# A two-layer streaming encoder on one core: the FFN's up product turned round, and GpSimd's preparation of the state-space matrices reordered

## The reference

```
for l in range(2):
    x = LN(alpha * x + 0.5 * swiglu(x, ffn1_w_up[l], ffn1_w_down[l]))
    x = LN(alpha * x + mixer(x, ...))            # state-space branch + sparse attention
    x = LN(alpha * x + 0.5 * swiglu(x, ffn2_w_up[l], ffn2_w_down[l]))

def swiglu(x, w_up, w_down):                     # w_up 1024 x 5632, w_down 2816 x 1024
    gate, up = split(x @ w_up, 2)
    return (silu(gate) * up) @ w_down

# state-space branch, per layer, 2048 complex states:
lam = min(lam_re, -1e-4) + i * lam_im ;  dt = exp(log_dt)
a_bar = exp(lam * dt) ;  b_bar = (a_bar - 1) / lam * b ;  c = c_re + i * c_im
states = scan(a_bar, b_bar @ u) ;  y = Re(c @ states) + d * u
```

## Time and profile before

| | |
|---|---|
| median of 3 runs | 1118.56 us (1118.28 to 1119.14) |
| profiled execution, from its first to its last instruction (span) | 1117.5 us |
| what the median has beside that span | 1.1 us |
| busy: TensorE, VectorE, ScalarE, GpSimd | 1105.8, 752.0, 561.1, 391.1 us |
| granted TensorE clock, mean | 0.999 |

### The profile page before, as it was taken

How to read it: one execution, slowest core, us unless ns; L and a number is a source line. 1 busy time by engine, 2 the same in 40 slices (tenths; PEclk the granted TensorE clock), 3 DMA queues, 4 the chain that set the end, 5 groups by cost and what they waited for, 6 DMA issues and landing times.

```text
span 1117.5 us, 17726 instructions
## 1 busy us (share of the span) xinstructions
PE 1105.8 (99%) x5979; PEld 917.9 (82%) x5979; DVE 752.0 (67%) x1073; ACT 561.1 (50%) x805; POOL 391.1 (35%) x560
## 2 busy tenths in 40 slices
PE   9999999999999999999999999999999999999997
PEld 7788888997788888888888888889877888888886
DVE  6657755789977865675575555467898787565544
ACT  6545433674873554543344544336748645453540
POOL 4889975107700188998500000011275000000001
PEclk9999999999999999999999999999999999999999
DMA  9776753644565577565367575536535666657541
GB/s 287 242 228 208 247 176 113 211 136 137 157 223 192 166 224 242 184 221 187 112 201 227 159 245 192 192 91 226 164 112 160 209 199 210 211 172 241 189 150 38
DMA packets 158655, 208.95 MB, mean 187 GB/s; under 512 B 12760, under 2 KB 107128, under 8 KB 158592
## 3 DMA queue, kind: packets, MB, share of 16 engines
q1 hardware_dynamic: 155232, 202.29, 56.7%
q10 hardware_dynamic: 2592, 3.67, 1.2%
q0 software_dynamic: 768, 2.17, 0.6%
HBM read 207.02 MB, written 1.06 MB: 186 GB/s over the span
## 4 chain that ended last, share of the span: by engine, by line
PE 82%; DVE 8%; ACT 3%; issue 3%; DMA 2%; SPq 1%; POOLq 0%; POOL 0%; DVEq 0%; ACTq 0%
PE ps L744 25%; PE ps L746 25%; PE ps L745 25%; DVE wlo L1246 4%; PE ps L768 2%; DMA raw<-in_ffn_w_up 1%; DVE score L1441 1%; ACT whi L430 1%; DMA raw<-in_w_in 1%; PE ps L758 1%; PE ps L986 1%; DVE gates L1413 1%; PE ps L1123 1%; PE ps L1125 1%; PE ps L1126 1%
## 5 line engine op out<-in xcount | busy, mean ns | idle before, releaser
L1246 DVE TENSOR_TENSOR wlo<-raw,whi 128x1024 fp32r<-128x1024 f32 (+1 forms) x371 | 475.7, 1298 | 188.4 <-ACT whi L430 174.2
L430 ACT CAST whi<-raw 128x1024 fp32r<-128x1024 f32 (+1 forms) x371 | 384.7, 1044 | 287.1 <-PE ps L746 225.2
L744 PE MATMUL ps<-whi,xh 128*128 128x512 f32 x976 | 384.4, 394 | 0.2 <-DVE wlo L1246 0.2
L746 PE MATMUL ps<-whi,xl 128*128 128x512 f32 x976 | 377.8, 387 | 0.0
L745 PE MATMUL ps<-wlo,xh 128*128 128x512 f32 x976 | 377.4, 387 | 0.0
L744 PEld LDWEIGHTS ps<-whi,xh 128*128 128x128 f32 x976 | 183.3, 188 | 39.0 <-issue 3.4
L746 PEld LDWEIGHTS ps<-whi,xl 128*128 128x128 f32 x976 | 183.2, 188 | 37.8
L745 PEld LDWEIGHTS ps<-wlo,xh 128*128 128x128 f32 x976 | 183.5, 188 | 34.9
L1671 POOL TENSOR_TENSOR rstd<-var_eps,cst 128x1 f32<-128x1 f32 x12 | 18.2, 1518 | 529.8 <-DVE var_eps L1295 520.7
L744 PE MATMUL ps<-whi,hh 128*128 128x512 f32 (+1 forms) x355 | 139.5, 393 | 0.0
L746 PE MATMUL ps<-whi,hl 128*128 128x512 f32 (+1 forms) x355 | 137.7, 388 | 0.0
(11 more groups left out here) (195 smaller groups left out, 1209.3 us busy)
## 6 DMA issues: line engine op xcount, KB each, us to landing
raw<-in_ffn_w_up SPq DMA_DIRECT2D x351, 256.0 KB, 4.0
raw<-in_ffn_w_down SPq DMA_DIRECT2D x176, 256.0 KB, 3.1
raw<-in_w_in SPq DMA_DIRECT2D x128, 256.0 KB, 3.4
raw<-in_w_branch SPq DMA_DIRECT2D x32, 256.0 KB, 3.3
raw<-in_w_out SPq DMA_DIRECT2D x32, 256.0 KB, 3.8
bias_g<-bias_rows ACTq DMA_DIRECT2D x16, 192.0 KB, 3.7
raw<-in_w_in SPq DMA_DIRECT2D x16, 148.0 KB, 2.3
affine<-in_ln_g SPq DMA_DIRECT2D x4, 512.0 KB, 5.6
```

Source lines behind the costliest of these rows:

```text
L430: nc.scalar.copy(whi[:, s % RING, 0:w], raw[:, s % RAW, 0:w]).then_inc(S["hi_done"], 1)
L744: nc.tensor.matmul(o, ah, bh, start=start, stop=False)
L746: return nc.tensor.matmul(o, al, bh, start=False, stop=stop)
L1246: nc.vector.tensor_tensor(wlo[:, s % RING, 0:w], raw[:, s % RAW, 0:w], f32(whi[:, s % RING, 0:w]), ALU.subtract).then_inc(S["split_done"], 1)
```

## The change

Three things are changed together.

1. From the third chunk on the up product has the weights as the stationary factor (`feature_chunk`). `xh` and `xl` lie next to each other as `x_hl`. A block of 128 columns of `whi` is multiplied with `xh` and `xl` at once (512 columns, the two products in the two halves of a PSUM bank), and the same block of `wlo` with `xh` alone (256 columns). The result has features in partitions, so that the transposes of h fall away in nine of eleven chunks. The two halves of a bank are added: ScalarE copies one half out (two copies), VectorE adds the other (two additions), then silu, product, high part and rest as before, on 512 elements at once. A chunk's result needs four banks, and TensorE begins chunk c when the rest of h of chunk c-2 is written (`h_split`).
2. In `prepare`, `gather_bias` stands behind the angles, b and c are loaded earlier, two quarters of b and all four of c are computed before the table, and the last two quarters of b after it. `b_bar` has two buffers. Twelve small products of the table are dropped in each layer (the squares are no longer scaled by one). VectorE's `clamp` stands at the head of the FFN, and its change of sign of c (`negate_c`) behind the third chunk instead of in the down product.
3. In the opening, the transposes of h of chunks 0 and 1 move into the third chunk, behind its first and third tile (`TURN_H`). Of the first FFN's chunk 0, both silus and both products stand ahead of the next four weight splits.

```
-                for c in range(2, PEEL):
-                    up_chunk(0, f, s0 + 4 * c, c, c % 2)
-                    h_transpose(f, c - 1, (c - 1) % 2, False)
+                for c in range(OLD_C, PEEL):
+                    feature_chunk(0, f, s0 + 4 * c, c, c % 2, c == OLD_C)
...
+            def feature_chunk(i, f, s, c, b, first=False):          # TensorE
+                if first:
+                    pe.wait_ge(S["h_ready"], 2 * by_tokens(f, 0) + NT)
+                else:
+                    pe.wait_ge(S["h_split"], steps(f, c - 2) + 1)
+                for q in range(4):
+                    wait_split(s + q, i)
+                    for kk in range(2):
+                        k = 2 * q + kk
+                        for g in range(2):
+                            for m in range(2):
+                                bank, at = UP_BANKS[b][g] + m, kk * 512 + g * CW + m * P
+                                nc.tensor.matmul(ps[:, bank, :], w(whi, s + q, at, at + P), x_hl[:, :, k, :],
+                                                 start=k == 0, stop=False)
+                                ins = nc.tensor.matmul(ps[:, bank, 0:SEQ], w(wlo, s + q, at, at + P), xh[:, k, :],
+                                                       start=False, stop=k == KT - 1)
+                    ins.then_inc(S["pe_used"], 1)
+                    if first and q in TURN_H:
+                        h_transpose(f, TURN_H[q])
...
@@ prepare_quarter @@
-                    pe.wait_ge(S["h_ready"], 2 * steps(f, NC_UP - 1) + NT)
+                    pe.wait_ge(S["h_split"], steps(f, NC_UP - 1) + 1)
...
+            def feature_chunk(i, f, s, c, b):                       # ScalarE
+                split_hi(i, s + RING)
+                split_hi(i, s + RING + 1)
+                act.wait_ge(S["pe_used"], used(s + 4) + RING * i)
+                nc.scalar.copy(silu[:, :, :], halves(b, 0)[1]).then_inc(S["gate_low"], 1)
+                act.wait_ge(S["h_split"], steps(f, c))
+                nc.scalar.copy(h[:, 0, :, :], halves(b, 1)[1]).then_inc(S["up_low"], 1)
+                act.wait_ge(S["gate_sum"], by_features(f, c) + 1)
+                nc.scalar.activation(silu[:, :, :], silu[:, :, :], ACT.Silu).then_inc(S["gate_silu"], 1)
+                split_hi(i, s + RING + 2)
+                act.wait_ge(S["up_h"], by_features(f, c) + 1)
+                nc.scalar.copy(hh[:, bass.ds(2 * c, 2), :], h[:, 0, :, :]).then_inc(S["hh_done"], 1)
+                split_hi(i, s + RING + 3)
...
@@ prepare, GpSimd @@
-                if l == 0:
-                    gather_bias()
...
                 op(m(5), m(4), k(12), ALU.add, S["angle_ready"])
+                pool.dma_start(b_raw[:, :, :, :], A["ssm_b_rows"][l]).then_inc(S["b_landed"], 16)
+                pool.dma_start(c_t[:, 0:2, :, :], A["ssm_c_rows"][l]).then_inc(S["c_landed"], 16)
+                if l == 0:
+                    gather_bias()
                 pool.wait_ge(S["sincos_ready"], l + 1)
...
+                pool.wait_ge(S["ct_ready"], l + 1)
+                prepare_b(0)
+                prepare_b(1)
+                for q in range(NQ):
+                    js = slice(4 * q, 4 * q + 4)
+                    cmul(c_t[:, 2, js, :], c_t[:, 3, js, :], col(11, js), col(12, js), c_t[:, 0, js, :],
+                         c_t[:, 1, js, :], -1, S["ca_ready"])
...
                     if n < HALF:
-                        square(m(21), m(22), m(18), m(19))
-                        op(m(18), m(21), k(14), ALU.mult)
-                        op(m(19), m(22), k(14), ALU.mult)
+                        square(m(then[0]), m(then[1]), m(now[0]), m(now[1]))
+                        now, then = then, now
+                prepare_b(2)
+                prepare_b(3)
```

More of the change, by code:

```diff
@@ L71 @@
 LOOP_I = (NC_UP - PEEL) // 2
+OLD_C = 2
+TURN_H = {0: 0, 2: 1}
 PAIR_IN = [(2, 0, 0), (2, 0, 3)]
@@ L167, in build @@
     b_raw = place("b_raw", [P, 2, NJ, 32])
-    b_bar = place("b_bar", [P, 4, P])
+    b_bar = place("b_bar", [P, 2, 4, P])
     tmp = place("tmp", [P, P])
@@ L1259, in x_lo, with h_lo, token_chunk @@
                                             ).then_inc(S["x_ready"], 1)
-            def h_lo(f, c, b):
+            def h_lo(f, c):
+                dve.wait_ge(S["hh_done"], steps(f, c) + 1)
+                k = slice(2 * c, 2 * c + 2)
+                nc.vector.tensor_tensor(hl[:, k, :], ps[:, 4 + c, :].rearrange("p (k n) -> p k n", k=2),
+                                        f32(hh[:, k, :]), ALU.subtract).then_inc(S["h_split"], 1)
+            def token_chunk(f, s, c):
+                for t in range(NT):
+                    dve.wait_ge(S["silu_done"], 2 * by_tokens(f, c) + t + 1)
+                    nc.vector.scalar_tensor_tensor(out=h[:, c, t, :], in0=silu[:, t, :], scalar=0.5,
+                                                   in1=ps[:, 2 * c + t, CW:2 * CW], op0=ALU.mult,
+                                                   op1=ALU.mult).then_inc(S["h_ready"], 1)
+                    if t == (1 if f == 0 and c == 0 else 0):
+                        for q in range(4):
+                            split_lo(0, s + RING + q)
+                if c > 0:
+                    h_lo(f, c - 1)
```

232 lines of the change are left out of this document (112 added, 120 removed).

## The result

The changed kernel took **1128.89 us** (median of 4 runs, 1124.22 to 1132.33) against 1118.6 of the kernel before beside it (1118.28 to 1119.14): ratio 1.0090, 95% interval 1.0071 to 1.0108. It is slower by about 10 us, where 1127 was predicted. Its runs lie 8 us apart, those of the kernel before 0.9; that had not been foreseen. It also lies 3.4 us above its own kernel's median, which matters wherever another kernel's trace is compared with it.

The account below looks back on a forecast made before the run. TensorE, busy 99% of the span, was taken as the bound. f = 0 +9.6, f = 1 +1.9, f = 2 and 3 -4.7 and clock +1.5 gave +8.3 us, about 1127 us; range 1115 to 1133.

Parts of the forecast that it names:

- the stall at quarter 2: Down product of f = 0: TensorE, wanting quarter 2 of b at 164.9, waits 12.1 us for GpSimd (3 to 17).
- the waits at quarter 0: TensorE waits for the last chunk's h_split before quarter 0 of b: 0.6 us in f = 0, 3 in f = 1.
- the clock: TensorE's clock halves after the 12 us idle in f = 0: +1.5 us.
- the up product: From the third chunk on: 11.10 us a chunk, fewer transposes; with the down product's -0.48, -2.34 us per FFN.
- the opening: Start of f = 0: the wait for h goes as the transposes come later, -0.82 us.
- f = 1: Second FFN: -2.34, plus 3.0 wait at quarter 0, plus 1.2 at quarter 2, together +1.9 us.
- GpSimd's ledger: GpSimd's steps in f = 0 summed from its start at 22.1: quarter 2 of b ready at 177 (168 to 182).
- the 2 us added for blocking: In GpSimd's sum for f = 0: VectorE's new product and rest hold GpSimd up, 2 us added.
- GpSimd is in time: Rival: quarter 2 of b comes before 164.9, no stall or clock loss; -6.6 us, 1112 us; chance 0.13.
- the two new instructions don't block: Rival: also b and c between their bounds, quarter 2 ready at 171.5, stall 6.6, 1118 to 1120 us; chance 0.12.
- The chain that outgrows a chunk: Rival: VectorE's chain takes 12.4 or more, 1.3 to 1.7 waited per chunk in f = 1; +5, 1132 us; chance 0.10.
- The fourth: Rival: up product's 256-column matmuls take 0.154 us instead of 0.120; +39, near 1166 us; chance 0.03.

Follow-up runs that it names:

- the old FFN: The kernel before, keeping its FFN and opening, with the changed preparation: 1124.45 us, ratio 1.0042.
- the last kernel: Changed kernel with bias early, c behind quarter 3 of b, bank wait at quarter 0, matmuls in pairs, no weight splits within the chain: 1109.45 us.
- the kernel with the filler: Changed kernel with 20 unread matmuls ahead of the waits at quarter 0 (f = 0 and 1) and quarter 2 (f = 0): 1128.24 us, ratio 1.0075.
- with pairs: The kernel with three edits, its chunk's matmuls reordered to two of 512 columns, then two of 256: 1118.48 us, ratio 0.9998.
- the kernel with three edits: Changed kernel with the bias early, the quarters of c behind quarter 3 of b, and the bank wait at quarter 0: 1119.2 us, ratio 1.0002.
- the changed FFN with the old preparation: Changed kernel with GpSimd's preparation in the order of before (bias, table, then quarters of b each followed by one of c): 1125.95 us, ratio 1.0057.

## Why the prediction came out as it did

The direction, the place and the size held. Inside, four terms were off: the stall at quarter 2 by 7 us one way, the waits at quarter 0, the clock and the up product the other way. In f = 0 they had to make up for each other, since the time at which GpSimd is ready ends the later wait however long the earlier one was; that the whole came within 2 us of the median is partly luck.

- **The up product and the opening.** Right in f = 0: 11.09 a chunk and the down product's start at 129.57, predicted 129.6 (its terms, 1.86 and 0.82, add up to 2.68 and not to 2.64). Wrong as a rule for all four: the step "I take 11.10" priced the mixed row of matmuls by two rows of unmixed ones, and the trace has a second pace of 11.31. f = 1 and 2 gained some 0.7 each by the up product instead of 2.3.
- **The wait at quarter 0.** This is the term that was mis-sized: 0.6 and 3, measured 5.2 and 5.1. Its own working, 8.4 against 8.3, gives 0.1 and, with four times 0.8, 3.3; the 0.6 has no row. The six steps and the splits within them were rightly listed. Unblocked it is 0.8 and 0.3. What failed is "I take a wait of 0.6 in f = 0": it let blocking into f = 1 only, because the 512-element part of the table begins at 134.7 in f = 0. The 256-element part before it blocks as well (two splits from 129.31 took 1.6 each instead of 1.22), and these splits ahead of the first sum, which I had not counted, were in the way until 132.4.
- **GpSimd's ledger.** Start 22.2 (22.1), b 68.2 (63.5), c 86.6 (83.8), table 103.0 (101.4), quarter 2 ready 175.9 (177). The angles took 14.6 instead of 10.5 and the small products 20.5 instead of 18.3, the bias 1.7 less; b, c and the table together 3.5 less. Without the 2 us added for blocking the terms give 174.9, 1.0 below what was measured; the sum came out better than its terms. The rule of the Trainium skill on two SBUF inputs ("SBUF — State Buffer", section "Who interferes with whom") was borne out: the product takes 0.68 with GpSimd idle and up to 1.77 beside it. With the old FFN quarter 2 is ready 4 us sooner (some of those 4 may be the new product's and rest's, some the opening's; this wasn't separated).
- **The stall at quarter 2.** 12.1 predicted, 4.8 measured, as TensorE came at 171.2 instead of 164.9: the wait at quarter 0 and its half clock had already spent the difference. With that wait removed it is 9.3 to 10.3. The two together, with clock, are what counts for f = 0: +10.8 measured, +11.1 predicted.
- **f = 1.** +5.4 instead of +1.9: 2.1 of the difference by the longer wait, 2.1 by a half clock that I had charged to f = 0 alone, 1.6 by the slow pace. Against that the stall of 1.2 at quarter 2 did not come, as GpSimd was ready at 539.3 and TensorE came at 549.3, and the waits in the first mixer are 1.2 shorter than in the profile before (0.2 in place of 1.4); those differ from profile to profile. f = 2 gave back 0.7 and f = 3 2.5, each predicted 2.3.
- **The clock.** 1.5 predicted for one stall, 5.8 measured for three; a gap of 5 us already costs 1.5 to 2.2.
- **The rivals.** That GpSimd is in time fell with 175.9. That the two new instructions don't block fell with 1.53 against 0.68, and on GpSimd's side with 1.59 against 1.29 for the same 512-element instruction beside them and without. The other half of that rival held: b took 9.2 and c 4.1 a quarter, between their bounds. How much of GpSimd's lateness is blocking by the new instructions no run separates. The chain that outgrows a chunk did not occur in the changed kernel's chunks, but appears as soon as the table stands beside them, 0.6 to 2.6 us a chunk. The fourth, 0.034 more for each matmul of 256 columns, is out; the slow pace adds 0.007 to a pair.

Why TensorE takes one pace or the other in an FFN stays open. It changes from FFN to FFN and between kernels that are alike up to that place; pairs of matmuls remove it. That it makes part of the spread of 8 us is an inference from the last kernel, which in pairs and without stalls spreads 1.1, and from the kernel with the filler, which alternates, has its clock whole (0.998 or more in all five runs) and spreads 3.5. It can't be all of it: the slowest run, the profiled one, has two FFNs at the fast pace already, so that the pace explains 3.3 us at most of the 8.1 to the fastest. The mean granted clock differs too, 0.991 in the slowest and 0.994 in the fastest run, an estimated 3 us. The rest is open.

## What to carry to other kernels

When a change makes one list longer ahead of a deadline and another chain longer ahead of the same consumer, price them in series: what the first wait takes, the second no longer does, and taking one away shows the other in full. Before crediting an engine with slack, ask what stands ahead of its critical step in its own order; moving work that isn't waited for out of the chain was worth more here than any saved instruction (1118.48 us with pairs, 1109.45 with this edit added). Put a wait where its data are used, and judge an edit of 5 us by the length of the stage it touches when whole runs spread by 8.

## What the runs showed of the hardware

Alternating matmuls of 512 and 256 columns, each with its own weights, run at one of two steady paces for a whole FFN, 346.6 or 353.4 ns a pair (11.09 and 11.31 us for 32). In groups of two and two it is 348.4 in all four. A gap of 5.2 us brought half clock for 3.4 us of work behind it, one of 4.8 for 4.8 us; a gap of 2.3 at the down product's start was followed by half clock in f = 1 of the kernel with three edits and not in f = 0 of it. In the kernel with pairs both gaps of 2.4 were followed by it, and in the changed FFN with the old preparation those of 2.6 and 2.7 but not that of 2.0. What these cost is what the steps say: 1.5 us behind the gap of 5.2, 2.2 behind the one of 4.8. Beside GpSimd's instructions on 256 to 512 elements VectorE's product and rest with both inputs in SBUF last 1.53 us instead of 0.68, and a sum with one input in PSUM keeps 0.68 (at 132.44, beside a GpSimd instruction on 256 elements).
